# Splitting the last whole weight half of the expert loop, and moving the down bias out of it

## The chip, the cores and the metric

One core of a Trainium2 chip runs the whole kernel. The metric is the device time of one execution in microseconds (us), the median of several runs. The engines are named as the profile does: PE is the tensor engine, DVE the vector engine, ACT the scalar engine, POOL is GpSimd, SP is SyncE, which issues most DMAs.

## What is computed

Two transformer blocks on 512 tokens of width 1024. The first has two attentions and a gated MLP, the second has two more mixers, a mixture of experts and a last gate. The change lies in the mixture of experts, which takes some 1200 of the 2480 us:

```
logits = xt @ w_router + b_router
top_vals, top_idx = lax.top_k(logits, TOP_K)          # 4 of 32 experts
gates = jax.nn.softmax(top_vals, axis=-1)
# tokens sorted by expert into blocks of 128
def expert_block(args):
    xb, e = args
    hgu = xb @ w_up_gate[e] + b_up_gate[e]            # 1024 -> 2048
    x_glu = jnp.minimum(hgu[:, :D_EXPERT], SWIGLU_LIMIT)
    x_lin = jnp.clip(hgu[:, D_EXPERT:], -SWIGLU_LIMIT, SWIGLU_LIMIT)
    hact = x_glu * jax.nn.sigmoid(SWIGLU_ALPHA * x_glu) * (x_lin + 1.0)
    return hact @ w_down[e] + b_down[e]               # 1024 -> 1024
ys = lax.map(expert_block, (xs, block_e)).reshape(n_slots, d)
return jnp.zeros((t, d), xt.dtype).at[slot_tok].add(ys * slot_gate[:, None])
```

All tensors are fp32.

## The kernel before

The program is written by hand, engine by engine; each engine runs its own list in order and waits on semaphores. Nothing is scheduled by a tool.

**The expert loop.** Tokens are sorted into slots of up to 128 rows for one expert. With these inputs there are 33 slots: slot 0 stands ahead of the loop, 32 rounds follow (`Fori(1, nb)`), and the down product of the last slot behind it. Round i does the up product of slot i and the down product of slot i - 1. The weights come in halves: one half is 512 rows by 512 columns, 1 MB, loaded by one DMA into one of twelve `stage` buffers. Halves 0 to 7 are the four column chunks of `w_up_gate`, halves 8 to 11 the two of `w_down`.

**Split products.** A product of two fp32 tensors is made of three fp32r matmuls: high x high (line L1732), high x low (L1733, with the weight's low part) and low x high (L1734). For each half ACT copies `stage` into `w_hi`, rounded to fp32r (`split_hi`, L1237), DVE subtracts it and writes the rest, `w_lo`, over `stage` (`split_lo`, L2405), and PE reads both, 12 matmuls of 512 columns (`fill`, L1718). There are six `w_hi` buffers (`TOPS`); `top_of` gives half number n of the split ones buffer n mod 6. The rows of tokens are split too: `xeT` is the input of the up product, `eaT` that of the down product, each with a part hi (ACT, L1228) and a part lo (DVE, L2519).

**The whole half.** Half 8 is not split (`WHOLE`, L38). PE takes it from `stage` in true fp32, 4 matmuls (L1726; the profile records each as two), and needs an unrounded copy of half of the rows, `ea_whole` (ACT, L1227).

**Biases.** Each `fill` begins with a bf16 matmul (L1721) that adds the bias of the slot's expert: `hot`, a row that marks the expert (DVE, `hot_row`, L2522), times `bias3`, the biases of all experts in three bf16 parts. `hot[0]` serves the up product, `hot[1]` the down product. The scaled result `ey` is added into `moe_sum` in HBM by an indirect DMA from POOL (L880); the rows of the next slots are gathered by another (L876).

**Order in a round.** PE: up chunk 0, turn (transpose) `ea`, chunks 1 and 2, find (the matmuls that look up the rows of slot i + 2), chunk 3, turn `rows`, down. ACT and DVE each have a fixed order of halves, activations and row parts (L1272 to L1283, L2542 to L2561). SP reloads a stage as soon as PE has read it (`half_done`, L667).

**Ahead of the loop.** Router, top 4, gates (`gate_of`), the place of each token in its slot (`rank`), find for slot 0, gather. Meanwhile DVE makes the table of slots (L2493 to L2501).

Of the kernel before, what the change touches and what calls it, by code (L numbers as in the profile page):

```python
# [37 lines left out]
WHOLE = 8  # L38
SPLIT = [h for h in range(HALVES) if h != WHOLE]
# [51 lines left out]
def program(nc, g, out):  # L91
# [138 lines left out]
    bsum = at(R, [NE, 3 * D], name="bsum")  # L230
    brem = at(R + 12 * KB, [NE, 3 * D], name="brem")
# [15 lines left out]
    ea_whole = at(R + 68 * KB, [P, KT // 2, P], name="ea_whole")  # L247
# [4 lines left out]
    bias3 = at(R + 82 * KB, [3 * NE, 3 * D], BF, name="bias3")  # L252
# [30 lines left out]
    hot = [take_T([3 * NE, P], BF, name=f"hot{i}") for i in range(2)]  # L283
# [409 lines left out]
    with nc.Block() as block:  # L693

        @block.sync
        def _(sp):
# [1965 lines left out]
```

## Time and profile before

| | us |
|---|---|
| median of 3 runs (2481.96 to 2489.38) | 2482.79 |
| profiled execution | 2481.1 |
| its span, first to last instruction | 2478.9 |
| PE busy | 2299.5 (93%) |
| DVE busy | 1817.4 (73%) |
| ACT busy | 1337.7 (54%) |
| POOL busy | 148.2 (6%) |
| L1726, the fp32 half: 256 records (8 a round, 32 rounds) | 115.1 |

A busy share is an average over a kernel whose stages have different limits; what matters here are the loop's own shares, in the rows below. Matmul records overlap each other, so the pace of matmuls is read from their starts, not from their length. The same holds for neighbouring DVE and ACT instructions, to a lesser degree. Idle time is given in square brackets before a row, with the instruction that ended it.

### The profile page before, as it was taken

To read this page: it belongs to the slowest core of one execution; us is meant where nothing else is said; L and a number is where in the kernel's file an instruction comes from. 1 tells how busy PE (TensorE), PEld (TensorE's weight loads), DVE (VectorE), ACT (ScalarE), POOL (GpSimd) and SP (SyncE) were. 2 spreads that over 40 slices of the span, in tenths; PEclk is the share of its full clock that TensorE was granted. 3 is DMA by queue.
4 is the path that set the end of the run, shared out by engine and by line. 5 is a ranking of instruction groups with operands and counts; after the bars stand their busy time and mean duration, and the time that the engine had idled before them with its cause. 6 is when DMAs were issued, how large, how long until landed. Compare 5 with 4: busy or idle time off the path is not lost.

```text
span 2478.9 us, 30772 instructions
## 1 busy us (share of the span) xinstructions
PE 2299.5 (93%) x10488; PEld 1816.5 (73%) x10488; DVE 1817.4 (73%) x2195; ACT 1337.7 (54%) x1529; POOL 148.2 (6%) x102
## 2 busy tenths in 40 slices
PE   5998988999998998585899999999999999999998
PEld 3866676888787876564677777777777777777776
DVE  7887545555425748566789889889889889889875
ACT  4355524334314435113576776776776776677663
POOL 1000000000000000001010110110110011011010
PEclk8999798999999999587899999999999999999999
DMA  9520222332112201125899999999999999999980
GB/s 322 191 102 27 93 68 68 102 102 94 68 60 83 102 35 48 46 74 222 303 364 376 370 367 371 373 367 375 370 368 374 371 367 372 370 370 366 376 284 34
DMA packets 286304, 569.86 MB, mean 230 GB/s; under 512 B 10492, under 2 KB 34975, under 8 KB 286207
## 3 DMA queue, kind: packets, MB, share of 16 engines
q1 hardware_dynamic: 273615, 523.69, 58.2%
q0 software_dynamic: 12624, 45.28, 6.6%
q8 instruction: 43, 0.70, 0.1%
q14 instruction: 22, 0.18, 0.0%
HBM read 542.71 MB, written 26.23 MB: 230 GB/s over the span
## 4 chain that ended last, share of the span: by engine, by line
PE 86%; DVE 7%; ACT 3%; issue 2%; DMA 1%; SPq 1%; DVEq 0%; POOL 0%; ACTq 0%
PE bank L1732 13%; PE bank L1734 13%; PE bank L1733 13%; PE bank L1392 6%; PE bank L1393 6%; PE bank L1394 6%; PE bank L1726 4%; PE bank L1373 4%; PE bank L1591 3%; PE bank L1592 3%; PE bank L1593 3%; PE bank L1721 2%; PE bank L1470 2%; PE bank L1452 1%; DMA x<-in_x 1%
## 5 line engine op out<-in xcount | busy, mean ns | idle before, releaser
L2405 DVE TENSOR_TENSOR w_lo<-stage,w_hi 128x2048 fp32r<-128x2048 f32 x364 | 816.6, 2286 | 49.0 <-ACT w_hi L1237 49.0
L1237 ACT ACTIVATE w_hi<-stage 128x2048 fp32r<-128x2048 f32 x364 | 685.5, 1911 | 203.5 <-PE bank L1734 199.9
L1732 PE MATMUL bank<-w_hi,xeT_hi 128*128 128x512 f32 x1056 | 439.0, 416 | 0.0
L1734 PE MATMUL bank<-w_hi,xeT_lo 128*128 128x512 f32 x1056 | 412.9, 391 | 0.0
L1733 PE MATMUL bank<-w_lo,xeT_hi 128*128 128x512 f32 x1056 | 412.8, 391 | 0.0
L1734 PEld LDWEIGHTS bank<-w_hi,xeT_lo 128*128 128x128 f32 x1056 | 199.1, 189 | 42.9
L1733 PEld LDWEIGHTS bank<-w_lo,xeT_hi 128*128 128x128 f32 x1056 | 199.5, 189 | 40.5
L1732 PEld LDWEIGHTS bank<-w_hi,xeT_hi 128*128 128x128 f32 x1056 | 200.5, 190 | 37.3
L1885 DVE TENSOR_TENSOR ring_low<-ring,half_top 128x2048 fp32r<-128x2048 f32 (+2 forms) x42 | 93.1, 2221 | 151.1 <-ACT half_top L971 150.8
L1394 PE MATMUL bank<-half_top,hT_low 128*128 128x512 f32 (+1 forms) x480 | 187.8, 391 | 0.0
L1732 PE MATMUL bank<-w_hi,eaT_hi 128*128 128x512 f32 x400 | 176.5, 441 | 0.0
L1392 PE MATMUL bank<-half_top,hT_top 128*128 128x512 f32 (+1 forms) x416 | 163.4, 393 | 4.0 <-DVE ring_low L1885 2.2
L971 ACT ACTIVATE half_top<-ring 128x2048 fp32r<-128x2048 f32 (+2 forms) x42 | 77.7, 1856 | 165.5 <-PE bank L1394 161.0
L1393 PE MATMUL bank<-ring_low,hT_top 128*128 128x512 f32 (+1 forms) x416 | 162.6, 391 | 0.0
L1734 PE MATMUL bank<-w_hi,eaT_lo 128*128 128x512 f32 x400 | 157.0, 392 | 0.0
L1733 PE MATMUL bank<-w_lo,eaT_hi 128*128 128x512 f32 x400 | 156.5, 391 | 0.0
L1591 PE MATMUL bank<-hT_hi,up_hi 128*128 128x512 f32 x352 | 137.8, 391 | 7.0 <-issue 7.0
L1592 PE MATMUL bank<-hT_lo,up_hi 128*128 128x512 f32 x352 | 137.6, 391 | 0.0
L1593 PE MATMUL bank<-hT_hi,up_lo 128*128 128x512 f32 x352 | 137.4, 390 | 0.0
L1253 ACT ACTIVATE ey<-bank,gates 128x512 f32<-128x512 f32 x64 | 44.2, 690 | 141.4 <-issue 114.7
L1726 PE MATMUL bank<-stage,ea_whole 128*128 128x512 f32 x256 | 115.1, 592 | 0.0
L880 POOL DMA_INDIRECT moe_sum<-ey,idx_out x32 | 50.7, 1583 | 1058.2 <-ACT ey L1253 1058.2
(449 smaller groups left out, 3782.6 us busy)
## 6 DMA issues: line engine op xcount, KB each, us to landing
stage<-in_w_up_gate SPq DMA_DIRECT2D x264, 1024.0 KB, 7.7
stage<-in_w_down SPq DMA_DIRECT2D x132, 1024.0 KB, 5.3
ring<-in_w_ada SPq DMA_DIRECT2D x12, 2048.0 KB, 9.5
ring<-in_w_up SPq DMA_DIRECT2D x22, 1024.0 KB, 7.7
ring<-in_w_in SPq DMA_DIRECT2D x10, 2048.0 KB, 7.9
ring<-in_w_out SPq DMA_DIRECT2D x4, 2048.0 KB, 12.8
ring<-in_w_down SPq DMA_DIRECT2D x4, 2048.0 KB, 8.1
stage<-in_w_ple_gate SPq DMA_DIRECT2D x4, 1024.0 KB, 7.4
```

Source lines behind the costliest of these rows:

```text
L1237: fn(w_hi[top_of(h)][:, :], src[:, :], ACT.Copy).then_inc(s_hi, 1)
L1392: mm(b, hi, wh, start=first, stop=False)
L1393: mm(b, hi, wl, start=False, stop=False)
L1394: return mm(b, lo, wh, start=False, stop=last)
L1591: mm(b[:, :], wh, hTs[0][:, k, :], start=k == 0, stop=False)
L1592: mm(b[:, :], wh, hTs[1][:, k, :], start=False, stop=False)
L1593: ins = mm(b[:, :], wl, hTs[0][:, k, :], start=False, stop=k == KT - 1)
L1726: ins = mm(bank[b][:, :], whole[:, k, :], wv[:, k, :], start=False, stop=False)
L1732: mm(bank[b][:, :], hi[:, kk, :], wh[:, k, :], start=False, stop=False)
L1733: mm(bank[b][:, :], hi[:, kk, :], wl[:, k, :], start=False, stop=False)
L1734: ins = mm(bank[b][:, :], lo[:, kk, :], wh[:, k, :], start=False, stop=kk == KT - 1)
L2405: tt(w_lo[h][:, :], stage[h][:, :], w_hi[top_of(h)][:, :].bitcast(FP), ALU.subtract).then_inc(s_lo, 1)
```

## The change

1. Half 8 is split like the others: the fp32 branch of `fill`, `ea_whole` and its copy are gone; ACT has a twelfth `w_hi` copy a round, DVE a twelfth `w_lo`. The half number modulo six now is the same in every round.
2. The down bias leaves the loop. `fill` for the down product begins with its first split matmul; the second `hot` row on DVE is gone. Instead, ahead of the loop, PE turns the gates of all tokens (`gatesT`) and multiplies them with `b_down`, 8 fp32 matmuls over 32 rows (`down_bias`, behind find for slot 0); ACT copies the results to `bdg`, and POOL adds them into `moe_sum` by 4 DMAs of 512 KB between its first two gathers. SP loads `b_down` behind the router, and waits for the four DMAs before its first loads of the loop; POOL waits for them before the loop.
3. The biases in three bf16 parts are those of the up product only, so DVE has a third less to do there. The gates' remainders go to `eqk`, so that `gate_of` stays whole.

The activation between the two products, `glu` and `glu_parts`, is the same in both. The core of the diff:

```diff
...
 HALVES = 2 * CHUNKS_E
-WHOLE = 8
-SPLIT = [h for h in range(HALVES) if h != WHOLE]
+SPLIT = list(range(HALVES))
 TOPS = 6
...
     pp = at(R + 32 * KB, [P, NT, D], name="pp")
-    bsum = at(R, [NE, 3 * D], name="bsum")
-    brem = at(R + 12 * KB, [NE, 3 * D], name="brem")
+    bsum = at(R, [NE, 2 * D], name="bsum")
+    brem = at(R + 12 * KB, [NE, 2 * D], name="brem")
     btmp = at(R + 66 * KB, [NE, D], name="btmp")
...
     product(("rank",))
+    product(("gT",), 6)
+    for t in range(NT):
+        for n in range(2):
+            product(("bd", t, n), (4, 5, 0, 2, 1, 3, 4, 5)[2 * t + n])
     uses = [0] * 8
...
             full(sp, ("router",))
+            sp.wait_ge(s_hn[0], 16 * NT // 2)
+            sp.dma_start(bdn[:, :], v["b_down_2"][0]).then_inc(s_bdn, 16)
             sp.wait_ge(s_slots, 1)
+            sp.wait_ge(s_acc, 32 * NT)
             nb = n_slots(sp)
...

-            for i in range(2):
-                pool.wait_ge(s_idx, i + 1)
-                gather()
+            pool.wait_ge(s_idx, 1)
+            gather()
+            for t in range(NT):
+                for n in range(2):
+                    taken(pool, ("bd", t, n))
+                pool.dma_start(acc_d[t * P:(t + 1) * P, :], bdg[:, t, :], accum_op=ALU.add).then_inc(s_acc, 16)
+            pool.wait_ge(s_idx, 2)
+            gather()
+            pool.wait_ge(s_acc, 32 * NT)
             pool.wait_ge(s_slots, 1)
...
             split_hi(0, 4, 5)
+            take(fn(gatesT[:, :], full(act_e, ("gT",))[0:NE, :], ACT.Copy), ("gT",))
+            for t in range(NT):
+                for n in range(2):
+                    take(fn(bdg[:, t, n * CW:(n + 1) * CW], full(act_e, ("bd", t, n))[:, :], ACT.Copy), ("bd", t, n))
             tiles_T(xeT, FU[6] + 1, FU[7] + 2)
...
                 split_hi(i, 4, 5, 6, 7)
-                tiles_T(eaT, 2 * i + (FU[6] + 1), 3 * i + (FU[7] + 3), ea_whole)
-                split_hi(i, 9)
+                tiles_T(eaT, 2 * i + (FU[6] + 1), 3 * i + (FU[7] + 3))
+                split_hi(i, 8, 9)
                 glu_parts(i, 0)
...
             publish(ins, ("rank",))
+            pe.wait_ge(s_gates, 1)
+            b = acquire(("gT",))
+            for t in range(NT):
+                ins = tr(b[0:NE, t * P:(t + 1) * P], gate_of[:, t, :])
+            publish(ins, ("gT",))
+
+            def down_bias():
+
+                taken(pe, ("gT",))
+                pe.wait_ge(s_bdn, 16)
+                for t in range(NT):
+                    for n in range(2):
+                        b = acquire(("bd", t, n))
+                        publish(mm(b[:, :], gatesT[:, t * P:(t + 1) * P], bdn[:, n * CW:(n + 1) * CW], start=True, stop=True), ("bd", t, n))

...

-            def fill(b, lhs, hot_, bcol, i, h0, whole=None):
+            def fill(b, lhs, bcol, i, h0):

                 hi, lo = lhs
-                mm(bank[b][:, :], hot_[:, :], bias3[:, bcol:bcol + CW], start=True, stop=False)
+                if bcol is not None:
+                    mm(bank[b][:, :], hot[:, :], bias3[:, bcol:bcol + CW], start=True, stop=False)
                 for h in (h0, h0 + 1):
-                    if whole is not None and h == WHOLE:
-                        wv = half_in(pe, i, h)[:, :].rearrange("p (k n) -> p k n", k=KT // 2)
-                        for k in range(KT // 2):
-                            ins = mm(bank[b][:, :], whole[:, k, :], wv[:, k, :], start=False, stop=False)
-                    else:
-                        pe.wait_ge(s_lo, split_no(i, h))
-                        wh, wl = (a[:, :].rearrange("p (k n) -> p k n", k=KT // 2) for a in (w_hi[top_of(h)], w_lo[h]))
-                        for k in range(KT // 2):
-                            kk = h % 2 * (KT // 2) + k
-                            mm(bank[b][:, :], hi[:, kk, :], wh[:, k, :], start=False, stop=False)
-                            mm(bank[b][:, :], hi[:, kk, :], wl[:, k, :], start=False, stop=False)
-                            ins = mm(bank[b][:, :], lo[:, kk, :], wh[:, k, :], start=False, stop=kk == KT - 1)
+                    pe.wait_ge(s_lo, split_no(i, h))
+                    wh, wl = (a[:, :].rearrange("p (k n) -> p k n", k=KT // 2) for a in (w_hi[top_of(h)], w_lo[h]))
+                    for k in range(KT // 2):
+                        kk = h % 2 * (KT // 2) + k
+                        mm(bank[b][:, :], hi[:, kk, :], wh[:, k, :], start=bcol is None and kk == 0, stop=False)
+                        mm(bank[b][:, :], hi[:, kk, :], wl[:, k, :], start=False, stop=False)
+                        ins = mm(bank[b][:, :], lo[:, kk, :], wh[:, k, :], start=False, stop=kk == KT - 1)
                     ins.then_inc(half_read[h // 2] if h == h0 else bank_full[b], 1)
...
                 pe.wait_ge(bank_taken[c], TK[c] + i)
-                fill(c, xeT, hot[0], c * CW, i, 2 * j)
-
-            def down(i, at_, h0, k6, k7, whole):
+                fill(c, xeT, c * CW, i, 2 * j)
+
+            def down(i, at_, h0, k6, k7):

                 pe.wait_ge(bank_taken[6], k6)
                 pe.wait_ge(bank_taken[7], k7)
-                pe.wait_ge(s_hotd, i + 1)
                 for n in range(2):
                     pe.wait_ge(bank_taken[4 + n], TK[4 + n] + i)
-                    fill(4 + n, eaT, hot[1], 2 * D + n * CW, at_, h0 + 2 * n, whole)
+                    fill(4 + n, eaT, None, at_, h0 + 2 * n)

...

-            dve.wait_ge(s_bsum, 32)
-            for c in range(3):
-                if c == 2:
-                    low(("wout2", 1), 0)
+            dve.wait_ge(s_bsum, 16)
+            for c in range(2):
                 part_ = slice(c * D, (c + 1) * D)
...
             dve.nop().then_inc(s_route, 1)
+            dve.nop().then_inc(s_gates, 1)
             parts3 = [found3[:, :, 3 + k * NE:3 + (k + 1) * NE] for k in range(3)]
             for k in range(3):
-                link(ve.tensor_copy(parts3[k], gate_of[:, :, :]))
+                left = eqk if k else gate_of
+                link(ve.tensor_copy(parts3[k], left[:, :, :]))
                 if k < 2:
-                    link(tt(gate_of[:, :, :], gate_of[:, :, :], parts3[k], ALU.subtract))
+                    link(tt(eqk[:, :, :], left[:, :, :], parts3[k], ALU.subtract))
             def build(s_, i):
...
             rest_T(xeT, 2)
-            hot_row(hot[0], 1, s_hotu)
+            hot_row(hot, 1, s_hotu)
             split_lo(1, 2, 3)
             nb = n_slots(dve)
             with dve.Fori(1, nb) as i:
                 split_lo(i, 4, 5)
                 rest_T(eaT, 4 * i)
                 build(i + 2, i + 2)
-                dve.wait_ge(bank_full[5], i + (FU[5] - 1))
-                hot_row(hot[1], i - 1, s_hotd)
-                split_lo(i, 6, 7, 9)
+                split_lo(i, 6, 7, 8, 9)
                 glu(i, 0)
...
                 rest_T(xeT, 4 * i + 2)
-                hot_row(hot[0], i + 1, s_hotu)
+                hot_row(hot, i + 1, s_hotu)
                 dve.wait_ge(s_scat, 16 * i)
                 dve.wait_ge(s_gate, 2 * i)
                 ve.tensor_copy(idx_out[:, :], idx_all[:, bass.ds(i - 1, 1)]).then_inc(s_ix, 1)
                 split_lo(i + 1, 2, 3)
             rest_T(eaT, 4 * nb)
-            dve.wait_ge(bank_full[5], nb + (FU[5] - 1))
-            hot_row(hot[1], nb - 1, s_hotd)
             link(ve.tensor_copy(idx_f[:, 2:3], idx_all[:, bass.ds(nb - 1, 1)]))
...
```

On PE, the down product in the loop. `fill` began so (a bias row, the fp32 half, then half 9):

```order
L1721 MATMUL bank<-bias_219_267,hot_242_290 128x512
L1726 MATMUL bank<-stage_180_228,ea_whole_261 128x512 x4
L1728 REGISTER_ALU
L1732 MATMUL bank<-w_hi_198_246,eaT_hi_258 128x512
L1733 MATMUL bank<-w_lo_193_241,eaT_hi_258 128x512
```

and begins now so (half 8 in `w_hi_198` and `w_lo_192`; L1758 to L1760 are the three split matmuls):

```order
L1778 REGISTER_ALU
L1754 REGISTER_ALU
L1758 MATMUL bank<-w_hi_198_246,eaT_hi_258 128x512
L1759 MATMUL bank<-w_lo_192_240,eaT_hi_258 128x512
L1760 MATMUL bank<-w_hi_198_246,eaT_lo_259 128x512
```

The bias matmul and the four fp32 matmuls are gone, and twelve split ones stand there.

On DVE, between the rows' low part `eaT_lo` and the activation, from the instruction `pick` on. Before:

```order
L2453 TENSOR_TENSOR pick_264<-conc_268,rank_276 128x512
L2546 REGISTER_ALU
L2522 ISA
L2522 TENSOR_SCALAR hot_242_290<-conc_268,slot_f_280 96x128
L2404 REGISTER_ALU
L2405 TENSOR_TENSOR w_lo_190_238<-stage_178_226,w_hi_196_244 128x2048
L2404 REGISTER_ALU
L2405 TENSOR_TENSOR w_lo_191_239<-stage_179_227,w_hi_197_245 128x2048
L2404 REGISTER_ALU
L2405 TENSOR_TENSOR w_lo_193_241<-stage_181_229,w_hi_198_246 128x2048
```

Now:

```order
L2480 TENSOR_TENSOR pick_263<-conc_270,rank_278 128x512
L2429 REGISTER_ALU
L2430 TENSOR_TENSOR w_lo_190_238<-stage_178_226,w_hi_196_244 128x2048
L2429 REGISTER_ALU
L2430 TENSOR_TENSOR w_lo_191_239<-stage_179_227,w_hi_197_245 128x2048
L2429 REGISTER_ALU
L2430 TENSOR_TENSOR w_lo_192_240<-stage_180_228,w_hi_198_246 128x2048
L2429 REGISTER_ALU
L2430 TENSOR_TENSOR w_lo_193_241<-stage_181_229,w_hi_199_247 128x2048
```

The `hot` row is gone, and the low part of half 8 (`w_lo_192`) stands between those of halves 7 and 9.

On PE ahead of the loop, between `rank` and the first expert:

```order
L1389 MATMUL bank<-cona_62,gate_of_277 32x128 x4
L1738 MATMUL bank<-found_216_264,pick_263 128x99 x4
L1730 MATMUL bank<-bdn_267,gatesT_268 128x512 x8
L1389 MATMUL bank<-cona_62,rows_254 128x128 x8
L1738 MATMUL bank<-found_216_264,pick_263 128x99 x4
```

The first and the third row are new: the turn of the gates, and the eight matmuls of the down bias ahead of the turn of the gathered rows.

## Rows read from the trace of the kernel before

**Rows 1.** One round: PE, PEld, DVE, ACT, POOL busy, PEclk, DMA share, GB/s.
```profile
1512.63:1549.44 36.81, 36.81 (x167) 28.58 (x167) 32.54 (x32) 26.45 (x22) 3.83 (x2) 1.00 1.04 367
```

**Rows 2.** The chain of waits, 1400 to 1800 us: shares of the stretch by line.
```profile
by line: PE bank L1732 27.3%; PE bank L1734 27.2%; PE bank L1733 27.2%; PE bank L1726 9.4%; PE bank L1373 4.8%; PE bank L1721 3.7%; PE bank L1708 0.6%
```

**Rows 3.** The timeline of TensorE over one down product: start us, us, instruction.
```profile
1500.51 0.38 PE L1721 MATMUL bank<-bias,hot 96*128 96x512 bf16 x1
...
1504.39 0.39 PE L1733 MATMUL bank<-w_lo,eaT_hi 128*128 128x512 f32 x1
...
1506.93 0.39 PE L1721 MATMUL bank<-bias,hot 96*128 96x512 bf16 x1
...
1507.40 0.39 PE L1733 MATMUL bank<-w_lo,eaT_hi 128*128 128x512 f32 x1
...
1512.63 0.39 PE L1721 MATMUL bank<-bias,hot 96*128 96x512 bf16 x1
```

**Rows 4.** The timeline of DVE over one round.
```profile
1509.89 4.52 DVE L2405 TENSOR_TENSOR w_lo<-stage,w_hi 128x2048 fp32r<-128x2048 f32 x2 [0.31 <-ACT w_hi L1237]
1515.44 4.49 DVE L2405 TENSOR_TENSOR w_lo<-stage,w_hi 128x2048 fp32r<-128x2048 f32 x2 [1.04 <-ACT w_hi L1237]
1521.82 1.29 DVE L2519 TENSOR_TENSOR eaT_lo<-bank,eaT_hi 128x512 fp32r<-128x512 f32 x2 [1.88 <-ACT eaT_hi L1228]
...
1524.50 0.28 DVE L2522 TENSOR_SCALAR hot<-conc,slot_f 96x128 bf16<-96x128 f32 x1
1524.70 6.69 DVE L2405 TENSOR_TENSOR w_lo<-stage,w_hi 128x2048 fp32r<-128x2048 f32 x3
...
1544.87 1.28 DVE L2519 TENSOR_TENSOR xeT_lo<-bank,xeT_hi 128x512 fp32r<-128x512 f32 x2
1546.06 0.27 DVE L2522 TENSOR_SCALAR hot<-conc,slot_f 96x128 bf16<-96x128 f32 x1
```

**Rows 5.** The timeline of ACT at the start of the same round.
```profile
1513.51 7.31 ACT L1237 ACTIVATE w_hi<-stage 128x2048 fp32r<-128x2048 f32 x4
1520.72 0.58 ACT L1227 ACTIVATE ea_whole<-bank 128x512 f32<-128x512 f32 x1
1521.19 1.08 ACT L1228 ACTIVATE eaT_hi<-bank 128x512 fp32r<-128x512 f32 x2
```

**Rows 6.** DMA rate in two stretches, DMA view, issues on SyncE's queue.
```profile
1488.00:1505.00 17.00, 17.00 (x77) 12.65 (x76) 16.80 (x16) 10.30 (x10) 0.00 (x0) 1.00 1.05 387
...
1480.30:1483.30 3.00, 3.00 (x19) 2.55 (x18) 2.82 (x2) 3.00 (x3) 1.48 (x1) 1.00 1.06 223
...
DMA packets 6627, 13.64 MB, mean 369 GB/s; under 512 B 223, under 2 KB 223, under 8 KB 6627
...
stage<-in_w_up_gate SPq DMA_DIRECT2D x88, 1024.0 KB, 8.1
...
1479.13 21.21 SPq L788 DMA_DIRECT2D stage<-in_w_up_gate  x8
```

**Rows 7.** Timelines of TensorE and DVE and the stretch view, ahead of the loop.
```profile
1168.35 0.49 PE L1708 MATMUL bank<-found,pick 128*128 128x99 bf16 x4 [1.76 <-DVE pick L2453]
1183.08 0.51 PE L1708 MATMUL bank<-found,pick 128*128 128x99 bf16 x4 [4.47 <-DVE xeT_lo L2519]
...
1181.75 1.27 DVE L2519 TENSOR_TENSOR xeT_lo<-bank,xeT_hi 128x512 fp32r<-128x512 f32 x2
...
1183.00:1186.00 3.00, 2.92 (x11) 2.35 (x12) 3.00 (x3) 0.00 (x0) 0.00 (x0) 0.50 0.00 0
```

**Rows 8.** Timelines of TensorE and DVE at the loop's end.
```profile
2396.15 1.03 PE L1373 MATMUL bank<-cona,ea 128*128 128x128 f32 x8
2399.55 0.39 PE L1721 MATMUL bank<-bias,hot 96*128 96x512 bf16 x1 [2.37 <-DVE hot L2522]
...
2397.84 1.28 DVE L2519 TENSOR_TENSOR eaT_lo<-bank,eaT_hi 128x512 fp32r<-128x512 f32 x2
2399.04 0.27 DVE L2522 TENSOR_SCALAR hot<-conc,slot_f 96x128 bf16<-96x128 f32 x1
```

More of the change, by code:

```diff
@@ L246, in program @@
     ey = at(R + 64 * KB, [P, D], name="ey")
-    ea_whole = at(R + 68 * KB, [P, KT // 2, P], name="ea_whole")
     el = [at(R + (72 + 2 * i) * KB, [P, CW], name=f"el{i}") for i in range(2)]
@@ L251, in program @@
     last_hot = at(R + 80 * KB, [P, S], name="last_hot")
-    bias3 = at(R + 82 * KB, [3 * NE, 3 * D], BF, name="bias3")
+    bias3 = at(R + 82 * KB, [3 * NE, 2 * D], BF, name="bias3")
+    bdn = at(R + 70 * KB, [NE, D], name="bdn")
+    gatesT = at(R + 66 * KB, [NE, S], name="gatesT")
+    bdg = at(80 * KB, [P, NT, D], name="bdg")
     conc = at(R + 88 * KB, [P, packs["c"][1]], name="conc")
@@ L282, in program @@
     idx_out = take_T([P, 1], I32, name="idx_out")
-    hot = [take_T([3 * NE, P], BF, name=f"hot{i}") for i in range(2)]
+    hot = take_T([3 * NE, P], BF, name="hot")
     nb_i = take_T([P, 1], I32, name="nb_i")
@@ L572, in program @@
     s_route, s_slots, s_b3 = sem("routes"), sem("slot_table"), sem("expert_bias_split")
-    s_pick, s_idx, s_got, s_hotu, s_hotd = (sem(n) for n in (
-        "pick_built", "gather_index", "rows_gathered", "hot_up", "hot_down"))
+    s_pick, s_idx, s_got, s_hotu, s_gates = (sem(n) for n in (
+        "pick_built", "gather_index", "rows_gathered", "hot_up", "gates_of_experts"))
     s_scat = sem("scattered")
+    s_bdn = sem("down_bias_in")
     s_back = [sem(f"sum_back{t}") for t in range(NT)]
@@ L774, in _ @@
             sp.dma_start(conc[:, :], v["consts"][:, packs["c"][0]:packs["c"][0] + packs["c"][1]]).then_inc(s_conc, 16)
-            sp.dma_start(bsum[:, 0:2 * D], v["b_up_gate_2"][0]).then_inc(s_bsum, 16)
-            sp.dma_start(bsum[:, 2 * D:], v["b_down_2"][0]).then_inc(s_bsum, 16)
+            sp.dma_start(bsum[:, :], v["b_up_gate_2"][0]).then_inc(s_bsum, 16)
             def expert(h, e, down):
@@ L1220, in _, with tiles_T @@
             norm(3, embedding)
-            def tiles_T(dst, k6, k7, whole=None):
+            def tiles_T(dst, k6, k7):
                 for j, (b, k) in enumerate(((6, k6), (7, k7))):
                     act_e.wait_ge(bank_full[b], k)
-                    if j == 0 and whole is not None:
-                        fn(whole[:, :, :], blk3(bank[b][:, :]), ACT.Copy)
                     fn(dst[0][:, 4 * j:4 * j + 4, :], blk3(bank[b][:, :]), ACT.Copy).then_inc(s_xhi, 1)
@@ L1762, in _ @@
             find(0, TK[7])
+            down_bias()
             pe.wait_ge(s_got, 16)
@@ L1782, in _ @@
                 turn(rows, 2 * i + (TK[6] + 1), 3 * i + (TK[7] + 4))
-                down(i - 1, i, 8, 2 * i + (TK[6] + 1), 3 * i + (TK[7] + 3), ea_whole)
+                down(i - 1, i, 8, 2 * i + (TK[6] + 1), 3 * i + (TK[7] + 3))
             turn_ea(nb - 1, 2 * nb + TK[6], 3 * nb + (TK[7] + 2))
-            down(nb - 1, nb, 0, 2 * nb + (TK[6] + 1), 3 * nb + (TK[7] + 3), None)
+            down(nb - 1, nb, 0, 2 * nb + (TK[6] + 1), 3 * nb + (TK[7] + 3))
             pe.wait_ge(s_lhot, 1)
@@ L2397, in _ @@
             dve.nop().then_inc(s_b3, 1)
+            low(("wout2", 1), 0)
             residual("wout2", None, (None, lambda: low(("wout2", 1), 1)))
@@ L2525, in _ @@
             build(1, 1)
-            hot_row(hot[0], 0, s_hotu)
+            hot_row(hot, 0, s_hotu)
             rest_T(xeT, 0)
```

## The prediction

> **What bounds the kernel now.** I read the busy shares by stretch first. In one round of the expert loop TensorE is busy for all 36.81 us at a granted clock of 1.00, the vector engine (DVE) for 32.54 us and the scalar engine (ACT) for 26.45 us, and the DMA share is over 1 [rows 1]. The loop has 32 rounds. The chain of waits between 1400 and 1800 us then names TensorE lines alone, and L1726, which is 4 fp32 matmuls a round, has 9.4% of it [rows 2]. So TensorE sets the round, and each microsecond taken from it is worth 32, until something else is late. Two things stand close behind: DVE, with its own order of work, and the DMA queue, which looks full. The prediction is decided there, so I read DVE's row of work over one round, what it waits for, and the rate of the DMA queue.
>
> **TensorE: what goes.** The down product begins at 1500.51 with its bias matmul and ends at 1512.63, where the next up product begins: 12.12 us [rows 3]. Inside it, from 1507.40 to 1512.63 stand 23 split matmuls, so 0.2274 us each. The bias matmul costs 0.24: 1506.93 to 1507.40 holds it and one split matmul. The piece from 1500.51 to 1504.39 is one bias matmul, the four fp32 matmuls and one split one, so the four cost 3.88 - 0.24 - 0.23 = 3.41 us, 0.853 each. After the change the down product is 4 halves of 12 split matmuls, 48 x 0.2274 = 10.92 us, without bias matmuls. It saves 12.12 - 10.92 = 1.20 us: 0.48 for two bias matmuls, and the rest for twelve cheap matmuls in place of four dear ones. TensorE's round becomes 35.61 us. Nothing else on TensorE changes in the loop.
>
> A rule of the Trainium skill stands close to this ("FP8 and Floating Point Precision", section "TensorE Precision Notes"): true fp32 takes four passes through the array. By it the four matmuls would cost 16 x 0.2274 = 3.64 us and the edit would be worth 0.23 us a round more, 7 us in all. The rows show 3.75 times a split matmul, and I go by the rows.
>
> **DVE: what is added.** DVE gets a twelfth w_lo subtraction a round. They stand 2.20 us apart where nothing is waited for (three in 6.69 with the last at 2.28, [rows 4]). It loses one hot row, 0.20 us (1524.50 to 1524.70). In the round of [rows 4] it waits 0.31, 1.04 and 1.88 us for ACT, 3.23 in all, so its work without waits is 36.81 - 3.23 = 33.58, and afterwards 33.58 + 2.20 - 0.20 = 35.58 us. That is 0.03 below TensorE's 35.61. The edit is free only if all three waits can be filled. I asked of each what holds it. Count from D, the end of the down product (1512.63). ACT starts four w_hi copies at D + 0.9, then ea_whole, then eaT_hi, and DVE's eaT_lo can start at D + 9.2 [rows 4, 5]. The ea_whole copy goes, worth 0.47 (1520.72 to 1521.19), so eaT_lo can start at D + 8.7. From there to the start of xeT_lo DVE needs 1544.87 - 1521.82 = 23.05 us, afterwards 25.05, then 1.2 to the hot row (1546.06), 0.27 for it, and 0.24 until TensorE goes on, as in the tail (hot row from 2399.04 to 2399.31, TensorE at 2399.55 [rows 8]). That is D + 35.5, and TensorE wants it at D + 35.61: it fits with 0.1 us left. The next eaT_lo would come at 8.7 + 35.58, again within TensorE's round. In this schedule DVE reaches the copies that it waited for later than they are made: half 4 at D + 4.2 where ACT had it at D + 2.8. So the 3.23 us are fillable, and I cost the DVE edit at nothing. If the cover is short, each microsecond of wait that stays is a microsecond a round. ACT gets 1.83 us for half 8 (four in 7.31) and loses 0.47; its busy 26.45 leaves room.
>
> **Slots of w_hi.** With twelve split halves on six slots each half waits for the half six before it. ACT comes to half 8 at about D + 9.3 and needs half 2, which TensorE has read at about D + 9.5 (6.5 for the first up product and the turn of ea, then 3). So 0.5 us of ACT's idle time is used, and nothing on the path.
>
> **The DMA queue.** A round moves 13.64 MB, nothing of which changes. Where only stage loads run it moves 387 GB/s; in the three microseconds with gather and scatter 223 [rows 6]. Bounds for the queue's own round: all at 387 gives 35.25 us, with the dip added on top, 3 x (1 - 223/387) = 1.27, it gives 36.5. TensorE will ask for 35.61, inside these bounds. I take 35.9, the middle. Then the queue falls behind by 0.3 us a round, 9 us at the end. Cover: the last up load of the eight is issued at about 1500.0 (1479.13 + 21.21 - 0.4), lands 8.1 later, and ACT wants it at about 1518.9, the fourth of the block at 1513.51: 10.8 us of slack [rows 5, 6]. So the lag stays hidden nearly to the end. Ends: 0 us at a round of 35.6 or less, 32 x 0.9 - 10.8 = 18 us at 36.5. I charge 3.
>
> **Ahead of the loop.** TensorE gets four small transposes of the gates before find, and eight fp32 matmuls behind it. Their price with 32 rows is not in the trace; the nearest is 0.853 at full clock, and the granted clock here is 0.50, the lower of its two levels [rows 3, 7], so 8 cost 6.8 to 13.6 us from 1168.85. But for the turn of the rows TensorE only waits here: find(1) starts at 1183.08, behind DVE's xeT_lo at 1181.75, which waits for DVE's own slot table [rows 7]. The turn of the rows and ACT's copy behind the bias need some 3 us. At 6.8 nothing is seen, at 13.6 some 4 us. The work in a row should lift the clock on the way, so I take 0.5. Should TensorE then stay at the high level (2.4 GHz, not 1.2) into the first expert, which starts at the low one now [rows 7], some 3 us come back: the 12 matmuls of its first half cost twice 0.2274 at the low level. The four accumulating DMAs of 512 KB meet an empty queue. SP waits for them before its first loop load, which it could issue only at about 1186 anyway; a delay of a few us would fall into the slack of 10.8. The eight ACT copies run behind the matmuls, in ACT's idle time. The shorter split of the biases on DVE was behind TensorE's products: nothing.
>
> **The tail.** After the last round DVE came to eaT_lo at 2397.84, 1.7 us after D (2396.15), and TensorE went on at 2399.55 [rows 8]. In the new schedule DVE finishes halves 2 and 3 of the last product at about D + 4.2, so 2.5 later; 0.48 of bias matmuls and 0.20 of a hot row go. Net +1.8.
>
> **Sum**, against the profiled execution of 2481.1 us: 2481.1 - 32 x 1.20 (38.4) + 3 + 0.5 + 1.8 = 2448.0. The profiled execution stands 1.7 below the median of the runs (2482.79), so for a median I say 2449.
>
> **Rivals.**
> *DMA sets the round.* For it: a share over 1 in the whole round and 387 GB/s flat for 17 us. Against it: TensorE does not wait once, and loads land 8.1 us after issue with 10.8 to spare. At the upper bound of 36.5 it costs 18 instead of 3: 2464. The Trainium skill ("DMA: Bandwidth & Descriptors", section "Where 436 GB/s comes from") has the HBM side bind at about 358 GB/s; by that 13.64 MB would need 38.1 us, the loop would be DMA-bound already and the change worth nothing. The rows show 387, so I don't follow it to the end, but it is why this rival is the second.
> *DVE sets the round.* DVE has 0.03 us a round, and 0.1 to the next up product. If half a microsecond of its waits stays, the round is 36.1: 32 x 0.5 = 16 more, 2465.
> *Slower.* The three DVE waits stay as they are, because ACT makes its copies only as TensorE frees slots. Then the round is 36.81 + 2.00 = 38.8, 64 us more: 2545. It decides from the point where over 1.23 of the 3.23 us stay (35.58 + 1.23 = 36.81). Against it: before, DVE waited because it was early, and TensorE never waited for it.
> *No change*: losses in several places that I have at zero cancel the gain; the nearest is TensorE's waits for the new half 8. 2475 to 2490.
>
> **Numbers.** TensorE sets the round: 0.62, own range 2442 to 2457. DMA 0.17, DVE 0.12, slower 0.05, no change 0.04. 0.3% is 7.4 us, about what a measurement of this kernel can tell. So faster 0.91, same 0.04, slower 0.05. The range takes the first case and the middle of the next two: 2441 to 2466.
>
> **What would show it.** Right: rounds of 35.6 us; TensorE busy throughout; no fp32 line in the loop; 12 w_lo a round; DVE's waits under 0.2 us a round; loads landing later and later over the loop, by some 9 us at most. Wrong: TensorE waiting for w_lo or for the hot row (DVE), or ACT's w_hi waiting for a stage load (DMA), or a TensorE gap over 14 us between find(0) and find(1).

## The result

The changed kernel took 2466.65 us in the median of 4 runs (2462.93 to 2468.66), the kernel before 2484.66 (4 runs, 2481.96 to 2489.38). The ratio is 0.9928, with a 95% interval of 0.9912 to 0.9944: faster by 18 us, where 33 were forecast; the median lies just above the forecast range of 2441 to 2466. The profiled execution took 2462.93 us, with a span of 2461.1; before it was 2481.1 and 2478.9.

### The profile page after: what moved, and what is told of

Same layout as the page of the kernel before. It is cut to its first block, busy times and chain, and to the rows that moved or that the text cites. A ratio compares the mean times of both kernels' runs of the same rounds, so it can differ in the third digit from the quotient of the medians.

```text
span 2461.1 us, 31010 instructions
## 1 busy us (share of the span) xinstructions
PE 2289.2 (93%) x10570; PEld 1846.2 (75%) x10570; DVE 1868.5 (76%) x2187; ACT 1385.7 (56%) x1538; POOL 308.4 (13%) x106
## 4 chain that ended last, share of the span: by engine, by line
PE 55%; issue 18%; DVE 17%; ACT 6%; DVEq 2%; DMA 1%; SPq 1%; ACTq 0%; POOL 0%
DVE w_lo L2430 7%; PE bank L1408 7%; PE bank L1409 6%; PE bank L1410 6%; PE bank L1758 5%; PE bank L1760 5%; PE bank L1759 5%; PE bank L1607 3%; PE bank L1609 3%; PE bank L1608 3%; PE bank L1389 3%; ACT w_hi L1249 3%; DVEq L645 2%; PE bank L1486 2%; PE bank L1468 1%
## 5 line engine op out<-in xcount | busy, mean ns | idle before, releaser
L2430 DVE TENSOR_TENSOR w_lo<-stage,w_hi 128x2048 fp32r<-128x2048 f32 x396 | 883.0, 2283 | 5.7 <-ACT w_hi L1249 5.7
L1249 ACT ACTIVATE w_hi<-stage 128x2048 fp32r<-128x2048 f32 x396 | 743.8, 1912 | 152.8 <-PE bank L1760 150.9
L1758 PE MATMUL bank<-w_hi,xeT_hi 128*128 128x512 f32 x1056 | 439.0, 416 | 0.0
L1760 PE MATMUL bank<-w_hi,xeT_lo 128*128 128x512 f32 x1056 | 412.6, 391 | 0.0
L888 POOL DMA_INDIRECT moe_sum<-ey,idx_out x32 | 245.9, 7685 | 878.8 <-ACT ey L1265 851.7
L1760 PEld LDWEIGHTS bank<-w_hi,xeT_lo 128*128 128x128 f32 x1056 | 199.0, 188 | 42.9
L1759 PEld LDWEIGHTS bank<-w_lo,xeT_hi 128*128 128x128 f32 x1056 | 199.5, 189 | 40.3
L1758 PEld LDWEIGHTS bank<-w_hi,xeT_hi 128*128 128x128 f32 x1056 | 200.3, 190 | 37.2
L1758 PE MATMUL bank<-w_hi,eaT_hi 128*128 128x512 f32 x528 | 210.0, 398 | 4.2 <-DVE eaT_lo L2546 4.2
L1760 PE MATMUL bank<-w_hi,eaT_lo 128*128 128x512 f32 x528 | 206.7, 391 | 0.0
L1759 PE MATMUL bank<-w_lo,eaT_hi 128*128 128x512 f32 x528 | 206.5, 391 | 0.0
L1758 PEld LDWEIGHTS bank<-w_hi,eaT_hi 128*128 128x128 f32 x528 | 99.9, 189 | 24.1 <-issue 4.4
```

The costliest lines, as they stand in the source:

```text
L888: pool.indirect_dma_start(out=acc_d[:, :], out_offset=bass.IndirectOffsetOnAxis(ap=idx_out[:, 0:1], axis=0), in_=ey[:, :], in_offset=None, ...
L1249: fn(w_hi[top_of(h)][:, :], src[:, :], ACT.Copy).then_inc(s_hi, 1)
L1758: mm(bank[b][:, :], hi[:, kk, :], wh[:, k, :], start=bcol is None and kk == 0, stop=False)
L1759: mm(bank[b][:, :], hi[:, kk, :], wl[:, k, :], start=False, stop=False)
L1760: ins = mm(bank[b][:, :], lo[:, kk, :], wh[:, k, :], start=False, stop=kk == KT - 1)
L2430: tt(w_lo[h][:, :], stage[h][:, :], w_hi[top_of(h)][:, :].bitcast(FP), ALU.subtract).then_inc(s_lo, 1)
```

## The profile after

One round, from one down product's end (D) to the next, as in [rows 1]: PE, PEld, DVE, ACT, POOL busy, PEclk, DMA share, GB/s.

```profile
1513.45:1549.46 36.01, 35.84 (x170) 29.11 (x170) 34.34 (x32) 27.78 (x22) 8.82 (x2) 1.00 1.05 378
```

The round is 36.01 us, not 35.61, and TensorE is no longer busy in all of it. DVE went from 32.54 to 34.34. The chain of waits over 1400 to 1800 us, where [rows 2] had TensorE alone:

```profile
by line: issue 34.1%; DVE w_lo L2430 15.4%; PE bank L1760 10.4%; PE bank L1758 10.4%; PE bank L1759 10.3%; ACT w_hi L1249 5.8%; DVEq L645 4.3%; DVE el L2537 1.9%; PE bank L1389 1.8%; ACT eaT_hi L1240 1.6%; DVE el L2535 1.0%; DVE eaT_lo L254
```

It now runs over DVE's w_lo, ACT's w_hi and eaT_hi, and TensorE in turn ("issue" is time in which the engine at hand waited for nothing that the profile shows). That points to one cycle through three engines that sets the round. TensorE's timeline shows where it stops (compare [rows 3]):

```profile
1537.27 0.60 PE L1389 MATMUL bank<-cona,rows 128*128 128x128 f32 x4
1538.05 0.66 PE L1389 MATMUL bank<-cona,rows 128*128 128x128 f32 x4 [0.17 <-DVE picked L2487]
...
1549.46 0.39 PE L1752 MATMUL bank<-bias,hot 96*128 96x512 bf16 x1
```

The first two rows are the turn of the gathered rows, four transposes each. The second half, which goes to bank 7, starts 0.78 us behind the first, where 0.4 are work: `find` had put its product into bank 7, and DVE's copy `picked` has to take it out. Before, `picked` came 0.9 us ahead of the turn, and the turn was one group of eight with no gap:

```profile
1535.29 0.26 DVE L2460 COPY picked<-bank 128x99 f32<-128x99 f32 x1
...
1536.45 1.03 PE L1373 MATMUL bank<-cona,rows 128*128 128x128 f32 x8
```

DVE now, over the same round (compare [rows 4]):

```profile
1512.75 8.88 DVE L2430 TENSOR_TENSOR w_lo<-stage,w_hi 128x2048 fp32r<-128x2048 f32 x4
1522.15 1.29 DVE L2546 TENSOR_TENSOR eaT_lo<-bank,eaT_hi 128x512 fp32r<-128x512 f32 x2 [0.51 <-ACT eaT_hi L1240]
1524.34 0.69 DVE L2480 TENSOR_TENSOR pick<-conc,rank 128x512 bf16 x1 [0.90 <-issue]
1524.94 8.89 DVE L2430 TENSOR_TENSOR w_lo<-stage,w_hi 128x2048 fp32r<-128x2048 f32 x4
...
1535.54 2.28 DVE L2430 TENSOR_TENSOR w_lo<-stage,w_hi 128x2048 fp32r<-128x2048 f32 x1
1537.74 0.25 DVE L2487 COPY picked<-bank 128x99 f32<-128x99 f32 x1
...
1548.50 0.27 DVE L2549 TENSOR_SCALAR hot<-conc,slot_f 96x128 bf16<-96x128 f32 x1
```

And ACT, which stands ahead of `eaT_lo` (compare [rows 5]; ea_whole is gone):

```profile
1514.33 7.31 ACT L1249 ACTIVATE w_hi<-stage 128x2048 fp32r<-128x2048 f32 x4
1521.55 1.06 ACT L1240 ACTIVATE eaT_hi<-bank 128x512 fp32r<-128x512 f32 x2
```

Read as one cycle from D = 1513.45: ACT takes the last product of the round before, makes its four copies from D + 0.88 on and then eaT_hi, DVE starts eaT_lo at D + 8.70, ends `picked` at D + 24.54 (1537.99), and TensorE needs another 11.47 for half a turn and the down product (1549.46). 24.54 + 11.47 = 36.01. That is the round, with nothing left over.

Loads land later as the loop goes on, as forecast: those of w_up_gate issued in 1300 to 1336 took 8.2 us in the median, those in 2200 to 2272 10.9.

Ahead of the loop (compare [rows 7]), TensorE:

```profile
1173.80 14.02 PE L1730 MATMUL bank<-bdn,gatesT 32*128 32x512 f32 x16
1187.75 1.97 PE L1389 MATMUL bank<-cona,rows 128*128 128x128 f32 x8
1191.13 0.52 PE L1738 MATMUL bank<-found,pick 128*128 128x99 bf16 x4 [1.42 <-DVE xeT_lo L2546]
```

The eight bias matmuls, recorded as two each, take 14.0 us at a granted clock of 0.50, the upper bound of the forecast (13.6). And at the end (compare [rows 8]):

```profile
2377.81 1.03 PE L1389 MATMUL bank<-cona,ea 128*128 128x128 f32 x8
2383.02 0.79 PE L1758 MATMUL bank<-w_hi,eaT_hi 128*128 128x512 f32 x1 [4.17 <-DVE eaT_lo L2546]
2383.60 0.63 PE L1759 MATMUL bank<-w_lo,eaT_hi 128*128 128x512 f32 x1
```

TensorE waits 4.2 us for eaT_lo, and then its first 14 or so matmuls are 0.43 apart instead of 0.23, at the lower clock level (0.50). Before, the wait was 2.4 us, and some 8 matmuls behind it were 0.43 apart (0.58 granted in 2400 to 2404).

The two profiled executions differ by 17.8 us of span. Up to TensorE's first `rank` matmul, ahead of all work that the change put on TensorE, after is 5.0 later (1160.43 to 1165.47): the same instructions at another clock (between 300 and 350 us the granted clock is 0.97 before and 0.86 after). From there to the second up product of the first expert 1.7 are lost. From there to the last turn of ea it took 1204.47 us before (1191.68 to 2396.15) and 1179.39 after (1198.42 to 2377.81): 25.1 gained. To the products that add the last rows 17.56 before and 20.08 after: 2.5 lost. Behind them 2.0 gained, unchanged code again. 5.0 + 1.7 - 25.1 + 2.5 - 2.0 = -17.9.

## Experiments

Three theories. **A**: the cycle above, with `picked` as a missed deadline in mid-round. **B**: DVE's total work sets the round, in whatever order it stands. **C**: the DMA queue sets it. Since identical code ahead of the loop moves by up to 10 us between executions (last section), I go by the length of the rounds in the traces, start to start of the scatter `moe_sum<-ey` (31 in each trace), which mostly repeats to 0.1 us, and take the medians beside it. Where a single number is given for a kernel's rounds it is the usual one; the last few scatter by up to 0.2.

**picked earlier.** In DVE's loop of the changed kernel:

```diff
-                split_lo(i, 10)
                 e = found(i + 2, 3 * i + (FU[7] + 4))
                 index(i + 2, e, 3 * i + (TK[7] + 4), 16 * i + 32)
-                split_lo(i, 11)
+                split_lo(i, 10, 11)
```

> The changed kernel with one move in DVE's loop: picked and the row numbers made from it come before the w_lo of half 10 instead of behind it. Theory A (a deadline in mid-round is missed: picked, which frees bank 7 for TensorE's turn of the rows, ends 24.6 us after the down product's end D, and TensorE is there at D + 24.15): picked comes 2.2 us earlier, TensorE no longer waits, the round falls from 36.0 to its own 35.6 to 35.7, 32 x 0.3 to 0.4 = 10 to 13 us, a median of 2453 to 2457. Theory B (DVE's work with its fixed gaps adds up to 36.0 in a round, in whatever order) and theory C (the DMA queue needs 36.0): round 36.0, median 2466.

Measured: 2460.17 us (2455.7 to 2461.56, 4 runs), 0.9904 [0.9876, 0.9931] of before. Two rounds from its first half and two late ones (start us, us, instruction):

```profile
1512.52 8.31 POOL L888 DMA_INDIRECT moe_sum<-ey,idx_out  x1 [25.95 <-ACT ey L1265]
1548.09 8.31 POOL L888 DMA_INDIRECT moe_sum<-ey,idx_out  x1 [25.98 <-ACT ey L1265]
...
2156.90 8.97 POOL L888 DMA_INDIRECT moe_sum<-ey,idx_out  x1 [25.93 <-ACT ey L1265]
2193.09 9.02 POOL L888 DMA_INDIRECT moe_sum<-ey,idx_out  x1 [25.93 <-ACT ey L1265]
```

Eighteen rounds are 35.57, TensorE's own 35.6, and the thirteen that follow 36.08 to 36.31, 36.19 in the mean. In the late ones ACT's copies wait for loads:

```profile
2209.35 1.92 ACT L1249 ACTIVATE w_hi<-stage 128x2048 fp32r<-128x2048 f32 x1 [2.01 <-DMA stage<-in_w_down]
2213.18 1.92 ACT L1249 ACTIVATE w_hi<-stage 128x2048 fp32r<-128x2048 f32 x1 [1.91 <-DMA stage<-in_w_down]
```

A holds and B falls: DVE's work is the same and the round is 0.44 shorter. But behind A's bound stands C's, and so the median is 3 us above the range expected. If 36.19 is the queue's own round from the start, 18 x (36.19 - 35.57) = 11.2 us of lag are what the loads' slack could hide; the prediction had worked out 10.8. That the queue sets the late rounds is here read from the waits; the run with fewer bytes further down tests it on another kernel.

**Fewer bytes.** Half 5 of each expert in the loop is loaded to one half (that half of the weights is left out, the other part is read twice):

```diff
+                if h == 5 and not isinstance(e, int):
+                    sp.dma_start(stage[h][:, :].rearrange("p (k n) -> p k n", k=KT // 2)[:, 2:4, :], src[:, 2:4, :]).then_inc(stage_in[h], 16)
```

> The changed kernel with half 5 of each expert in the loop loaded to one half of its columns (0.52 MB of 13.64 a round less); ACT and DVE read that part twice, so their work and TensorE's is the same size (the kernel leaves out this half of the weights). Theory C (the queue sets 36.0): the queue needs 1.3 us less a round, so the round falls to TensorE's 35.6, 13 us, median 2453. Theories A and B: round 36.0, median 2466; only landing times get shorter.

Measured: 2462.31 us (2461.73 to 2468.85), rounds of 36.02 in the mean, as with all the bytes. C is not what sets the changed kernel's round.

**One more DVE instruction, ahead of picked and behind it.** `ts(pad[:, :], cc("iota"), 1.0, None, ALU.mult)`, once in front of `found`, once behind `index`.

> The changed kernel with one more DVE instruction a round (a product of 128x512 numbers by 1, written to an unused place, about 0.42 us like the first one of the activation), put right ahead of picked. Theory A (the way from the down product's end over eaT_lo to picked sets the round): the round grows by the whole of it, 36.0 to 36.4, 32 x 0.42 = 13 us, a time of about 2480. Theory B (DVE's total work sets it): the same, 2480. A TensorE or a DMA bound would hide it.

> The same extra DVE instruction as in the run with it ahead of picked, put behind the row numbers, ahead of the w_lo of half 11. Theory A: not on the way to picked. The hot row then ends 0.42 later, where 0.4 are free before the next up product, and DVE's wait of 0.5 ahead of eaT_lo takes up the rest: round 36.0 to 36.1, a time of 2463 to 2470. Theory B (DVE's total work, its place in the round does not matter): 36.4, about 2480.

Measured: ahead, rounds of 36.34 (median 2469.47, 2463.01 to 2479.25, 8 runs); behind, rounds of 35.91 (2462.00, 2452.62 to 2464.45, 3 runs). The same instruction costs 0.33 a round in one place (its step in DVE's row is 0.33, not the 0.42 said), and nothing 2 us later. B would have both alike. The median of the first is a weak witness: its 8 runs spread over 16 us, the profiled one was the longest (2479.25), and 10 us above the changed kernel, as the rounds say, would be 2476. Behind `picked` the round even gets 0.09 shorter. Its rows show that the gap ahead of pick is 0.78 there and not 0.90:

```profile
1523.52 1.29 DVE L2547 TENSOR_TENSOR eaT_lo<-bank,eaT_hi 128x512 fp32r<-128x512 f32 x2 [0.22 <-ACT eaT_hi L1241]
1525.60 0.69 DVE L2481 TENSOR_TENSOR pick<-conc,rank 128x512 bf16 x1 [0.78 <-issue]
```

**The two parts alone.** The bias alone moved (half 8 whole, `SPLIT` without it, `ea_whole` back):

> The changed kernel with half 8 of the down product whole again (four fp32 matmuls, eleven w_lo): the down bias alone is moved. Theory A: TensorE's round is 36.81 - 0.48 = 36.33; picked ends at about D + 22.9 and is wanted at D + 24.2, so nothing waits for it: round 36.33, 15 us gained in the loop, 1 to 2 lost ahead of it, median 2468 to 2470. Theory B (DVE work, here 33.4 without waits): 36.33 as well. Theory C (DMA queue at 36.0): 36.33 as well. All three would be wrong if the round were not 36.3.

Measured: 2469.05 us (2465.85 to 2472.32, 6 runs), 0.9944 [0.9926, 0.9963], rounds of 36.31. TensorE sets them, as said.

The split alone (the kernel before with `SPLIT = list(range(HALVES))` and no fp32 half):

> The kernel before with half 8 split like the others and the down bias left in the loop. TensorE's own round would be 36.81 - 0.72 = 36.09. Theory A: picked ends at D + 24.6 + 0.2 for the second hot row, and from there to the next D are the second half of the turn and the down product with its two bias matmuls, 11.4 + 0.48: round 36.7, so 0.1 to 0.2 gained a round, 3 to 5 us, 2 lost again in the tail: median 2479 to 2483. Theory B (DVE's total, 36.0 + 0.2): round 36.2, median about 2465. Theory C: 36.1, about 2462.

Measured: 2515.29 us (2513.99 to 2518.16), 1.0127 [1.0101, 1.0152], rounds of 37.73. Slower than before by 30 us, with 0.72 us less work on TensorE in every round. All three theories missed it: A had come nearest with rounds of 36.7, but had them shorter than before, not longer. The difference is one gap on DVE:

```profile
1533.84 1.29 DVE L2518 TENSOR_TENSOR eaT_lo<-bank,eaT_hi 128x512 fp32r<-128x512 f32 x2 [1.01 <-ACT eaT_hi L1227]
1537.19 0.69 DVE L2452 TENSOR_TENSOR pick<-conc,rank 128x512 bf16 x1 [2.06 <-issue]
```

It is 2.06 where the changed kernel has 0.90. Everything from there to `picked` is 1.16 later, and A's 36.7 with 1.16 on it is 37.9. TensorE waits 1.3 to 1.6 us for `picked` in each round. In this gap DVE's sequencer loads the two registers that `pick` is indexed with. The same kernel with `picked` earlier:

> The kernel before with half 8 split, the bias left in the loop, and picked moved ahead of the w_lo of half 10. The run with the split alone had rounds of 37.73, of which 1.1 came from a wait of 1.9 to 2.0 ahead of pick (0.8 to 0.9 in every other run) and the rest from picked being late. Theory A: picked 2.2 earlier covers both (it was 1.6 late): TensorE's round of 36.09 or the queue's of 36.17 sets the time: about 2464 to 2467. Theory B (DVE's total work): its work with the long wait ahead of pick is 36.8 to 37.1 with the wait for ACT filled: round 36.8 or more, 2485 or more.

Measured: 2466.70 us (2460.55 to 2468.6, 3 runs), 0.9922 [0.9895, 0.9949], rounds of 36.08, and the gap is 0.79 again:

```profile
1517.54 0.69 DVE L2452 TENSOR_TENSOR pick<-conc,rank 128x512 bf16 x1 [0.79 <-issue]
```

So the move of one line is worth 1.65 us a round here, 49 us by the medians, of which more than half is the gap that fell back, and what is left is TensorE's 36.09. The split alone is only worth having with it.

**The bias behind the loop.** Bias products into the banks that take the last expert's rows; nothing of it ahead of the loop:

```diff
             turn_ea(nb - 1, 2 * nb + TK[6], 3 * nb + (TK[7] + 2))
+            biased = {(t, n): down_bias(t, n) for t in range(2) for n in range(2)}
             down(nb - 1, nb, 0, 2 * nb + (TK[6] + 1), 3 * nb + (TK[7] + 3))
...
-                    publish(mm(b[:, :], last_hot[:, t * P:(t + 1) * P], ea[:, n * CW:(n + 1) * CW], start=True, stop=True), ("add", t, n))
+                    publish(mm(b[:, :], last_hot[:, t * P:(t + 1) * P], ea[:, n * CW:(n + 1) * CW], start=False, stop=True), ("add", t, n))
```

> The changed kernel with the eight down-bias matmuls moved behind the loop: no copies and no accumulating DMAs ahead of it; four are issued in TensorE's gap between the turn of ea and the last down product, four behind that product, and the last expert's rows are added in the same banks. Ahead of the loop the 3.0 us that find(1) came later go and the earlier rise of the clock (1.3) goes with them: 1.7 gained. Behind it four at 0.85 = 3.4 us fill a gap of 4.2, so TensorE may keep its high clock into the last down product (14 matmuls at the low level cost 0.2 more each, 2.8), and the other four cost up to 3.4, of which 1.0 falls into the wait for ACT. So -1.7 - 2.8 + 2.4 = -2 us, a median of 2462 to 2466; the rounds stay at 36.0.

Measured: 2459.34 us (2457.54 to 2464.87), 0.9905 [0.9873, 0.9938], rounds of 36.0. Most of the 7 us below the changed kernel can't be put down to the move: its first `rank` matmul, ahead of it, stands at 1158.00, 7.5 earlier than in the changed kernel. By stages the move itself gives 3.0 and takes 0.8 back ahead of the loop (find(1) 22.63 behind rank, not 25.66; 8.10 to the second up product, not 7.29), and costs 2.4 behind it: 22.52 from the last turn of ea to the adding products, not 20.08. The clock fell in the gap, though filled by matmuls:

```profile
2370.08 4.17 PE L1713 MATMUL bank<-bdn,gatesT 32*128 32x512 f32 x8
2374.23 0.79 PE L1742 MATMUL bank<-w_hi,eaT_hi 128*128 128x512 f32 x1
2374.81 0.63 PE L1743 MATMUL bank<-w_lo,eaT_hi 128*128 128x512 f32 x1
```

The granted clock is 1.00 in 2370.1 to 2372 and 0.50 in 2374 to 2378. The forecast gain of 2 is 0 by these rows. But the clock does not always fall there. In the kernel with all three moves (next) the bias has the same place, eaT_lo comes 1.3 us sooner behind the turn, and behind the same group of matmuls the clock stays at 1.00:

```profile
2370.18 3.69 PE L1713 MATMUL bank<-bdn,gatesT 32*128 32x512 f32 x8
2373.81 0.50 PE L1742 MATMUL bank<-w_hi,eaT_hi 128*128 128x512 f32 x1
```

What decides between the two no run shows.

**All three moves**, `picked` early, the bias behind the loop, and on ACT `split_hi(i, 4, 5, 6)`, `tiles_T(eaT, ...)`, `split_hi(i, 7, 8, 9)`:

> The changed kernel with picked moved ahead of the w_lo of half 10, ACT's eaT_hi moved ahead of its w_hi of half 7, and the down bias behind the loop. By the round times of the kernel with picked early alone (35.57 for 18 rounds, 36.17 from then on, when loads have become late) TensorE sets the first rounds and the DMA queue the rest. ACT's move shortens the way to eaT_lo by 1.5 more, which nothing waits for: no further gain in a round of 35.57. With the 2 us of the bias's place: 2460 - 2 = 2458. If ACT's or DVE's place did set the late rounds of 36.17 and not the queue, they would fall to 35.6 and the median to 2449.

Measured: 2457.03 us (2454.19 to 2464.55), 0.9899 [0.9864, 0.9934]. Rounds of 35.59 but for two of 40.2, in the 20th and 28th; in the first of these TensorE waits for the gathered rows:

```profile
1959.65 1.86 PE L1376 MATMUL bank<-cona,rows 128*128 128x128 f32 x8 [2.78 <-DMA rows<-hn_rows,idx_in]
```

The mean of 31 rounds is 35.89, against 35.83 with `picked` early alone and 36.02 in the changed kernel: the lag comes in two lumps instead of thirteen small steps, and costs the loop 2 us more than `picked` early alone. Is it the queue?

> The kernel with all three moves, and half 5 of each expert in the loop loaded to one half of its columns (0.52 MB of 13.64 a round less; that half of the weights is left out, the other part is read twice). If the DMA queue made the two rounds of 40.2 there, they go: all rounds 35.6, 9 us less, a time of about 2446. If they come from ACT's or DVE's order, they stay.

Measured: 2448.95 us (2448.2 to 2449.69, 2 runs), every round 35.6 (mean 35.59). It is: the same order of work on all engines, 0.52 MB less a round, and both lumps are gone. TensorE's 35.6 stands then through the whole loop.

The version without the bias's move, on one chip with the changed kernel:

> The changed kernel once more, on the same chip as the kernel with picked early and ACT's new order, as the mark for it. Rounds of 36.0, median 2463 to 2468.

> The changed kernel with picked moved ahead of the w_lo of half 10 and ACT's eaT_hi ahead of its w_hi of half 7; the down bias stays ahead of the loop. Theory A with the DMA queue as the next bound: rounds of 35.6 until the loads are late, then waits for stage loads, over the loop a mean of about 35.85: 5 us less than the changed kernel on the same chip. If ACT's order mattered beside picked's, the mean would be 35.6 and the gain 13 us.

Measured: the changed kernel 2466.08 (2462.27 to 2466.9), 0.9921 [0.9894, 0.9947]; with the two moves 2460.81 (2455.65 to 2463.89), 0.9897 [0.9867, 0.9926]. The medians differ by the 5 us that were expected, but the rounds do not bear them out, and the intervals overlap. The mean round is 36.01 with the two moves and 36.04 in the changed kernel, 1 us over the loop, where 35.85 was said. Twenty-eight rounds are near 35.6, and three, the 20th, 28th and 29th, take 40.3, 38.5 and 40.7; in each of them TensorE waits 2.7 us for the gathered rows. So ACT's move, which was to cost nothing, makes the loop 5 us longer than `picked` early alone: it shortens no round and turns the lag into lumps. The best version with the whole computation is so far the one with all three moves or the one with `picked` early, both about 2457 to 2461; these runs can't tell them apart. The loop is shortest with `picked` early alone.

## Why the prediction was off

- **TensorE's side** was right: 1.20 us less a round, and 35.57 to 35.59 where nothing else binds (35.61 said).
- **DVE is where it failed.** The step "So the 3.23 us are fillable, and I cost the DVE edit at nothing" was checked at one deadline, the hot row at D + 35.5 against 35.61. That one holds: the row starts at D + 35.05, and with its 0.27 and the 0.24 to TensorE's start that is D + 35.56, within the 35.61. With `picked` early it still holds, with nothing to spare: the row ends 0.21 us ahead of TensorE's start. The waits did fill: 3.23 us became 0.51. But on the way from eaT_lo to the hot row lies `picked`, in the line with `find(i + 2)` in bank 7, and TensorE wants bank 7 at about D + 24.25 (the turn begins at D + 23.82, half of it is 0.43). Before, `picked` ended at D + 22.9, 1.3 early. The change puts one w_lo (2.20) ahead of it, takes out the hot row (0.20) and ea_whole (0.47), and the gap ahead of pick grew by 0.12: 1.65 later, so 0.3 too late, and with TensorE's start behind the wait the round is 36.01 instead of 35.61. 32 x 0.40 = 12.8 us, which is all but 0.5 of the gap between 25.1 gained in the loop and the 38.4 of the forecast. The forecast's signs of being wrong named TensorE's waits for w_lo and for the hot row, not for `picked`. The rival "DVE sets the round" had nearly this size (16 us, 2465) at a chance of 0.12, for another reason: DVE's total, with half a microsecond of its waits left. The 0.51 us do stay ahead of eaT_lo, but as a result and not as the cause: they are gone as soon as `picked` comes early. It is the place that counts, as the instruction ahead of `picked` and behind it shows.
- **The DMA queue.** The forecast charged 3 us for a queue round of 35.9 with 10.8 of slack. The slack was about right (11.2 by the 18 rounds), the queue's round is 36.19, above the value taken and below the upper bound. In the changed kernel it cost nothing, since the round of 36.0 leaves a lag of 0.18 a round; with `picked` in time it would have cost some 8, not 3. Even the late rounds move the full 13.64 MB in 36.19 us, 377 GB/s. The Trainium skill ("DMA: Bandwidth & Descriptors", section "Where 436 GB/s comes from"), by whose HBM figure of about 358 GB/s such a round would need 38.1 us, is not borne out by them; here one core runs alone.
- **Ahead of the loop** +1.7 for +0.5. The forecast had the clock lifted on the way by the work in a row. It was not: the granted clock is 0.50 through all 14.0 us of the bias matmuls, and find(1) comes 3.0 later. Only in the first expert did it rise sooner, behind some 6 matmuls at the low level instead of 12, and gave 1.3 back (3 said). The other 5 us there are not the change's.
- **The tail** +2.5 for +1.8, near by luck in part. TensorE goes on 1.8 later behind the turn of ea, where 2.3 were in the sum; the 0.48 of bias matmuls go; and some 14 matmuls stand at the low clock level where 8 did before, about 1.1 us, which was not in the sum.

The forecast for a median should have read 2449.7, not 2449 (2448.0 + 1.7). With the terms as measured, 2481.1 - 38.4 + 12.8 + 1.7 + 2.5 = 2459.7 for the profiled execution, and 2462.7 with the 5.0 and 2.0 of unchanged code; measured 2462.9.

## What to carry to other kernels

When work is added to an engine with idle time, list every instruction behind it that another engine waits for, with the time at which it is wanted, and not only the last one before the loop closes: fillable idle time behind the deadline does not help the one ahead of it. An instruction with a deadline goes ahead of bulk work without one; here that swap made the split alone some 15 us faster than before instead of 30 slower (more than half of it through the gap ahead of `pick`, whose cause is open). And when a bound is lifted, ask how long the slack of the next one lasts: a queue that is 1.7% too slow shows only after 18 rounds.

## What the runs showed of the hardware

**GpSimd's scatter seems to be held up by DVE's w_lo.** Before, the scatter `moe_sum<-ey` took 1.58 us on POOL; after, 7.83:

```profile
1515.28 7.83 POOL L888 DMA_INDIRECT moe_sum<-ey,idx_out  x1 [26.88 <-ACT ey L1265]
```

It begins inside DVE's row of four w_lo and ends at 1523.11, 1.48 us behind the end of the last (1521.63). With `picked` early it is 8.31 and ends 1.47 behind the last w_lo; in the split alone 7.33, ending 1.46 behind it. Before, and with the bias alone (1.60), it fell into a pause of DVE between two w_lo. With all three moves ACT's order puts a pause of 0.32 us into DVE's row, and the scatter takes 2.13, again ending 1.46 behind the last w_lo ahead of the pause (1508.25):

```profile
1507.58 2.13 POOL L883 DMA_INDIRECT moe_sum<-ey,idx_out  x1 [31.46 <-ACT ey L1255]
```

So it seems to wait for DVE's row of w_lo to end and then takes its 1.5 us. DVE need not be idle for that: with `picked` early, eaT_lo, which reads one input from PSUM, starts 0.04 us behind the row. This is argued from where the ends fall in these four traces; no run was made to test it. It cost nothing here. The Trainium skill ("SBUF — State Buffer", section "Who interferes with whom") has DVE and GpSimd share a port pair, and a DVE instruction with two inputs in SBUF, as w_lo is, contend with a GpSimd instruction that reads SBUF. The scatter reads its row numbers, `idx_out`, from SBUF, and these rows agree. The Trainium skill infers there that the writing of descriptors is not stalled by such a DVE instruction; these rows can't tell whether it is.

**A gap for two register loads** ahead of `pick` was 0.5 to 1.1 us in thirteen traces and 1.8 to 2.1 in one (the split alone), mostly within 0.2 us over the rounds of a kernel, and back at 0.79 when DVE's order changed behind it. That the loads fill it is argued from the program: the profile shows nothing that DVE waits for. What sets its length stays open, and it was worth 1.1 us a round.

**Identical code ahead of the loop** reached the first `rank` matmul at 1160.43 us before, 1165.47 after, 1158.00 with the bias behind the loop and 1167.99 in the changed kernel's second trace, with other granted clocks on the way. A median of a few runs can't tell 3 us; the rounds of a trace can.
